# Moving one weight split of the next stage ahead of the last modulation product at the end of a feed-forward stage

## What is computed

```python
x = x + 0.5 * swiglu(rms_norm(x, ffn1_norm[l]), ffn1_w_gu[l], ffn1_w_down[l])
h = rms_norm(x, mix_norm[l])
z = h @ w_in[l]                                  # first stack
...
mod = silu_c @ w_ada[layer] + b_ada[layer]       # second stack: 9 * 1024 modulations
x = x + 0.5 * g1 * swiglu_2(h, ffn_w1[layer, 0], ffn_w3[layer, 0], ffn_w2[layer, 0])
h = modulate(rmsnorm(x, norm_g[layer, 1]), sh2, sc2)
proj = h @ w_in[layer]
```

## Time and profile before

| | |
|---|---|
| runs, median | 3187.64 us (3184.56 to 3193.06) |
| profiled execution, its own time | 3193.06 us |
| its span | 3191.4 us |
| TensorE matmuls busy | 94% of the span |
| VectorE busy | 67% |
| ScalarE busy | 40% |
| mean granted TensorE clock | 0.961 |
| number of tiles split | 438 |

### The profile page before, as it was taken

How to read it: one execution, slowest core, us unless ns; L and a number is a source line. 1 busy time by engine, 2 the same in 40 slices (tenths; PEclk the granted TensorE clock), 3 DMA queues, 4 the chain that set the end, 5 groups by cost and what they waited for, 6 DMA issues and landing times. The chain is left out here.

```text
span 3191.4 us, 54435 instructions
## 1 busy us (share of the span) xinstructions
PE 2994.2 (94%) x23232; PEld 2898.3 (91%) x23240; DVE 2142.7 (67%) x2745; ACT 1283.1 (40%) x1246; POOL 185.1 (6%) x174
## 2 busy tenths in 40 slices
PE   7999998999998999998989989998889999988899
PEld 7999998998998999898989989997689999976899
DVE  6677866555766678856556667676666666766666
ACT  4344434343334334344443324343533243445332
POOL 0000310000000000400000000002000000020000
PEclk9999999999998999999999998999889989998999
DMA  6654333443655644333435655653146556531464
GB/s 231 241 212 159 133 133 111 154 159 146 245 204 200 250 185 172 127 133 111 163 128 198 238 206 193 234 187 115 53 168 247 199 206 239 186 118 53 165 247 183
DMA packets 79822, 560.76 MB, mean 176 GB/s; under 512 B 8544, under 2 KB 11872, under 8 KB 12128
## 3 DMA queue, kind: packets, MB, share of 16 engines
q1 hardware_dynamic: 66912, 464.99, 40.2%
q0 software_dynamic: 12672, 92.28, 7.5%
HBM read 556.18 MB, written 1.05 MB: 175 GB/s over the span
## 5 line engine op out<-in xcount | busy, mean ns | idle before, releaser
L253 DVE TENSOR_TENSOR ring_lo<-ring,w_hi 128x2048 fp32r<-128x2048 f32 x438 | 1010.7, 2309 | 663.5 <-ACT w_hi L246 655.3
L259 PE MATMUL ps<-h_hi,w_hi 128*128 128x256 f32 x4688 | 1357.5, 290 | 39.8 <-DVE h_lo L1904 17.1
L259 PE MATMUL ps<-h_lo,w_hi 128*128 128x256 f32 x4688 | 1339.4, 286 | 0.0
L259 PE MATMUL ps<-h_hi,ring_lo 128*128 128x256 f32 x4688 | 1338.7, 286 | 0.0
L246 ACT ACTIVATE w_hi<-ring 128x2048 fp32r<-128x2048 f32 x438 | 835.9, 1909 | 738.0 <-PE ps L259 599.3
L259 PEld LDWEIGHTS ps<-h_hi,w_hi 128*128 128x128 f32 x4688 | 914.5, 195 | 52.6 <-issue 44.7
L259 PEld LDWEIGHTS ps<-h_lo,w_hi 128*128 128x128 f32 x4688 | 914.0, 195 | 7.1 <-issue 6.4
L259 PEld LDWEIGHTS ps<-h_hi,ring_lo 128*128 128x128 f32 x4688 | 913.1, 195 | 0.0
L259 PE MATMUL ps<-g_hi,w_hi 128*128 128x256 f32 x1408 | 398.5, 283 | 0.0
L259 PE MATMUL ps<-g_lo,w_hi 128*128 128x256 f32 x1408 | 398.5, 283 | 0.0
L259 PE MATMUL ps<-g_hi,ring_lo 128*128 128x256 f32 x1408 | 398.4, 283 | 0.0
(11 more groups left out here) (297 smaller groups left out, 3180.7 us busy)
## 6 DMA issues: line engine op xcount, KB each, us to landing
ring<-stream SPq DMA_DIRECT2D x438, 1024.0 KB, 4.8
e<-ada POOLq DMA_DIRECT2D x88, 1024.0 KB, 5.1
mem<-mem_t SPq DMA_DIRECT2D x1, 1024.0 KB, 6.2
con_sb<-con SPq DMA_DIRECT2D x1, 1024.0 KB, 8.3
x<-x_t SPq DMA_DIRECT2D x1, 1024.0 KB, 10.7
out_t<-x SPq DMA_DIRECT2D x1, 1024.0 KB, 4.5
con_sb<-con SPq DMA_DIRECT2D x1, 640.0 KB, 8.5
e<-lmask SPq DMA_DIRECT2D x1, 512.0 KB, 11.5
```

The source lines that it names most:

```text
L253: nc.vector.tensor_tensor(ring_lo[:, p % RING, :], ring[:, p % RING, :], w_hi[:, p % HIGHS, :].bitcast(F32), ALU.subtract).then_inc(S.w_lo ...
L259: mm = nc.tensor.matmul(out, a, b, start=start and n == 0, stop=stop and n == 2, skip_group_check=group)
```

## The change

In `ffn_dve` the third `low` is now issued in chunk 10 too, ahead of the last `ada_product`, where it is that of tile 34. The `low` of that tile which stood between `residual` and `norm_dve` is taken out, in both stacks. In the feed-forward stages at the end of a layer nothing changes: there tile 34 would lie behind the last tile of the stream, and `low` returns without an instruction. So one instruction moves in four places of an execution, one in each layer; these places are called seams below.

```diff
@@ -514,8 +514,7 @@
                 low(dve, block, p0 + t + HIGHS)
                 gated(i, t + 1)
                 low(dve, block, p0 + t + HIGHS + 1)
-                if i < CHUNKS - 1:
-                    low(dve, block, p0 + t + HIGHS + 2)
+                low(dve, block, p0 + t + HIGHS + 2)
                 ada_product(dve, l, layers, PER_FFN * f, i)
@@ -1075,7 +1074,6 @@
             residual(dve, ffn_banks(dve, FFN_A, 0), 4, 0.5,
                      lambda b: gains(dve, 4, v_now[:, V1_MIX:V1_MIX + KD], b))
-            low(dve, 1, MIX - 2 + HIGHS)
             norm_dve(dve, chain, 1)
@@ -1766,7 +1764,6 @@
             residual(dve, ffn_banks(dve, FFN_C, 0), 4, parts[2], lambda b: gains(dve, 4, parts[4], b))
-            low(dve, 2, Z_QI - 2 + HIGHS)
             norm_dve(dve, chain, 1, parts[3])
```

## The result

The changed kernel takes 3210.8 us in the median of four runs (3209.9 to 3211.6), against 3188.3 us before (3184.6 to 3193.1): ratio 1.0069, 95% interval 1.0052 to 1.0087, so 22.5 us slower where 25 had been forecast, within the range. The profiled execution has a span of 3210.5 us against 3191.4, a difference of 19.1; the profiled execution of before was the slowest of its runs, which is why the spans lie closer together than the medians.

A forecast was written before the change was run, and what follows sets the result against it. TensorE bounds the kernel, and at four seams waits for VectorE's chain. Queue delay 19.0, clock at the sums 3.0 and at the small matmuls 2.6, less at most 0.3: 25 us slower, 3212.6 us, range 3200 to 3226.

The forecast's parts named there:

- The place and the wait: VectorE, first seam: the moved split waits 3.6 us for tile 34's rounding, so the first residual is 5.85 us late.
- The slack: First-stack seams, ahead of TensorE's sums: some of the fourth residual's 5.65 us delay is free, leaving 4.5 us a seam.
- the 19.0 of the sum: Delay over the four seams at an unchanged clock: 2 x 4.5 + 2 x 5.0 = 19.0 us.
- The clock at the sums: TensorE's sums of squares at the seams run slower after idle time: 1.5 us a stack, 3.0 us added in all.
- The clock at the small matmuls: The 44 small matmuls at each seam lengthen from a mean of 6.23 us to 7.04: 2.6 us added in all.
- the upper bound: All four seams with the small matmuls at the lower clock, 10.7 us more, and the sums at their bounds: 36 us slower.
- The removal: Taking out the split of tile 34 ahead of the norm gives 0 to 0.3 us a seam.
- The signs that were named: At each seam: VectorE idle some 3.5 us (2.7 in the second stack) before the moved split; L475 4.5 to 6.5 us later.

The follow-up runs named there:

- e7: The changed kernel with 14 matmuls of zeros between tile 32 and the sums at the four seams, their result never read: 3200.4 us, ratio to before 1.0040.
- e1: The kernel before with the split of tile 34 moved from ahead of the norm to behind it at all four seams: 3188.6 us, ratio 0.9995.
- e3: The kernel before with VectorE made to wait for tile 34's rounding ahead of the last product, the split staying ahead of the norm: 3199.3 us, ratio 1.0032.
- e5: The kernel before with the right-hand side of the 44 small matmuls 128 columns wide in place of one: 3172.2 us, ratio 0.9951.
- e4: The changed kernel with the right-hand side of the 44 small matmuls 128 columns wide in place of one: 3193.0 us, ratio to before 1.0011.

## Why the prediction was right

**The place and the wait.** The rounding of tile 34 was to end at 1.92 us behind the end of tile 31 and hold VectorE for 3.6 us; it held it for 3.55. The first residual was to be 5.85 us late; it is 7.52 - 1.67 = 5.85. At the first seam of the second stack the wait was 3.38 us where 2.7 were named. The queue's order did it: the run with the wait alone and the run with the work alone each cost a part.

**The slack.** The fourth residual is 5.65 us late, the start of the small matmuls in the first stack only 4.75 with the clock kept up (e7), where 4.5 was worked out: the slack behind the fourth residual is 0.9 us and not 1.15. In the second stack the small matmuls are 4.98 and 5.42 late, where 5.0 and 5.2 were worked out. Together 19.9 against the 19.0 of the sum. This term is the mechanism of the forecast, and it makes up nearly all of the measured loss.

**The clock at the sums.** Put at 3.0 us, between bounds of 0 and 6. The changed kernel and the one with the pause filled differ by 2.6 us at the start of the small matmuls (1.7, 0.4, 0.6 and 0.0 at the four seams, where the forecast had about 0.95 and 0.55).

**The clock at the small matmuls.** This term had the wrong sign: 2.6 us was added, since they take 7.04 us at the starts of a layer. In the windows with L475 alone of the changed kernel they take

```profile
232.00:252.00 20.00, 6.90 (x44) 7.00 (x44) 0.61 0.04 17
1185.00:1200.00 15.00, 4.97 (x44) 5.07 (x44) 0.84 0.00 1
2140.00:2158.00 18.00, 6.84 (x44) 6.94 (x44) 0.75 0.00 1
2783.00:2800.00 17.00, 5.28 (x44) 5.38 (x44) 0.77 0.00 0
```

which is 24.0 us against 24.9 before. The forecast held that the clock falls once, ahead of or within the sums, and not within the small matmuls. In fact it fell in the pause or the sums, came back before the small matmuls at all four seams, and fell a second time: 2.7 and 2.8 us into them at the first and the third, about when they end at the second and the fourth. These windows of the changed kernel show it for the second and the third:

```profile
1187.00:1193.00 6.00, 6.00 (x50) 5.82 (x49) 3.59 (x7) 3.40 (x5) 0.00 (x0) 1.00 0.00 0
2143.00:2145.00 2.00, 2.00 (x20) 2.00 (x19) 1.35 (x4) 0.87 (x2) 0.00 (x0) 1.00 0.00 0
2145.00:2150.00 5.00, 5.00 (x27) 5.00 (x27) 4.59 (x10) 2.65 (x7) 0.00 (x0) 0.56 0.00 2
```

The starts of a layer were a poor neighbour to take, and one of the four was left out. In the first layer of the first stack, where idle time stands ahead of the sums as well, the small matmuls took 4.97 us in the kernel before:

```profile
29.00:38.00 9.00, 4.97 (x44) 5.07 (x44) 0.88 0.01 3
```

With it the mean over the starts is 6.52 and not 7.04, and the term 4 x 0.29 - 0.64 = 0.5 us in place of 2.6. At no seam was the clock low through the whole chain, which was the condition of the upper bound. With -0.9 in place of +2.6 the sum would have been 21 us, and with the 19.9 of e7 in place of 19.0, 22. The measured 22.5 has an interval of 17 to 28 us, so the measured time doesn't decide between these. That 25 came so near to 22.5 is in part luck: the small matmuls' term was 3.5 us too high, and the queue's delay 0.9 too low.

**The removal.** Forecast at 0 to 0.3 us a seam; e1 shows no difference that can be told from none.

**The signs that were named.** The idle time ahead of the moved split came, 3.55 and 3.38 us, and so did the split's absence ahead of L363 and the pause before the first L352 (3.4 us). L363's wait is 3.41, 2.13, 2.31 and 1.83 us at the four seams; the first lies a little over the 1.5 to 3 that were named, and the sums took longest there. The small matmuls start 5.1 to 6.4 us late, inside the 4.5 to 6.5.

In a sentence apart: the Trainium skill, "TensorE: Matmul & The Clock Gate", Part 1, the section on the array's architectural detail, has VectorE as a strict first-in first-out engine, and e3 agrees with it: the product started 3.64 us late behind a wait that neither it nor the residuals needed, and the execution took 10 us longer.

## What to carry to other kernels

Before an instruction moves up in an in-order queue, look up when its operand is ready, not only whether the engine has work for it there: what stands behind it pays the wait, and here that was the chain on which the core's next stage hung. An instruction that sits in front of a longer wait for another engine can be free: this split was, and taking it away won nothing (e1). And read the granted clock across each seam: here 22 very narrow matmuls, at eight places of an execution, gave 17 us back when they were made wide, nearly as much as the four moved instructions cost. To price an edit by a trace, compare the stretches that it touches, not the whole span.

## What the runs showed of the hardware

I had not expected that widening 44 small float32 matmuls from 1 column to 128 would cost 0.1 us each time and win 17 us over the kernel (3172.2 against 3188.9 on that chip; mean granted clock of the profiled executions 0.970 against 0.961). In the profiled executions the gain is 20.9 us: 8.7 in the seams (87.3 against 96.0 in the table) and 11.2 between the small matmuls at the four starts of a layer and the seam that follows. At each of these eight places the kernel before has a fall of the clock to 0.50 within the small matmuls or right behind them, though TensorE's timeline shows no pause there, and with 128 columns none has: e5 spends no time at 0.50 in its seams, against 31 us, and in e4 the clock falls only in the pause ahead of the sums or at their start. Why the number of columns matters to the clock these runs don't say.
